# A transformer block on one core: output and second feed-forward products with tokens on the partitions, as seven block products, and normalizations along rows

## What is computed

```python
mixed = (g_pool * y_pool + g_rwkv * y_rwkv) @ w_out[l]
x = layer_norm(ALPHA * x + (1 + gt1) * mixed, ln1_g[l], ln1_b[l], LN_EPS).astype(x.dtype)
h = x * (1 + sc2) + sh2
f = jnp.square(jax.nn.relu(h @ w_ff1[l])) @ w_ff2[l]
x = layer_norm(ALPHA * x + (1 + gt2) * f, ln2_g[l], ln2_b[l], LN_EPS).astype(x.dtype)
```

## Time and profile before

| | us |
|---|---|
| median of 3 runs | 1109.46 |
| range of the runs | 1108.66 to 1114.62 |
| profiled execution | 1106.47 |
| its span, first to last instruction | 1104.7 |
| TensorE busy in the span | 999.9 |
| DVE, ACT, POOL busy | 517.9, 413.8, 401.8 |
| mean granted TensorE clock | 0.957 |

### The profile page before, as it was taken

How to read it: one execution, slowest core, us unless ns; L and a number is a source line. 1 busy time by engine, 2 the same in 40 slices (tenths; PEclk the granted TensorE clock), 3 DMA queues, 4 the chain that set the end, 5 groups by cost and what they waited for, 6 DMA issues and landing times.

```text
span 1104.7 us, 25425 instructions
## 1 busy us (share of the span) xinstructions
PE 999.9 (91%) x10997; PEld 798.8 (72%) x10997; DVE 517.9 (47%) x620; ACT 413.8 (37%) x500; POOL 401.8 (36%) x236
## 2 busy tenths in 40 slices
PE   1898998898899889997999999889999999999992
PEld 1676777685677678675688888768888888888881
DVE  6636589377748768743231245746112112112217
ACT  0335354356335532524433224375124224214311
POOL 6333412311311131125253443445434434443422
PEclk9799999999999899998899999879999999999996
DMA  9322333223323324321433543304333333333201
GB/s 370 106 77 63 97 117 102 79 79 94 93 79 98 103 60 118 105 76 39 133 100 101 160 114 107 95 1 132 97 94 97 96 96 91 99 95 93 79 1 76
DMA packets 153641, 108.08 MB, mean 98 GB/s; under 512 B 5395, under 2 KB 145601, under 8 KB 153537
## 3 DMA queue, kind: packets, MB, share of 16 engines
q1 hardware_dynamic: 143729, 83.46, 25.9%
q10 hardware_dynamic: 9808, 23.08, 6.9%
HBM read 100.23 MB, written 2.10 MB: 93 GB/s over the span
## 4 chain that ended last, share of the span: by engine, by line
PE 47%; DVE 4%; DMA 1%; ACT 1%; issue 0%; SPq 0%; POOL 0%; DVEq 0%; ACTq 0%; POOLq 0%
PE set L1757 23%; PE bank L1757 20%; PE bank L1859 1%; PE set L1859 1%; DVE G L1319 1%; DMA w_raw<-in_w_rwkv_up_dram 1%; DVE xt L1388 1%; DVE xt L1390 1%; PE set L1821 0%; DVE t L1304 0%; PE set L1838 0%; PE set L1607 0%; PE set L1606 0%; DVE aa L1322 0%; DVE stat L1348 0%
## 5 line engine op out<-in xcount | busy, mean ns | idle before, releaser
L560 POOL TENSOR_TENSOR w_lo<-w_raw,w_hi 128x1024 fp32r<-128x1024 f32 (+2 forms) x87 | 200.4, 2303 | 439.2 <-ACT w_hi L641 399.2
L616 POOL TENSOR_TENSOR w_lo<-w_raw,w_hi 128x1024 fp32r<-128x1024 f32 x48 | 115.8, 2413 | 145.9 <-ACT w_hi L936 145.7
L1460 PE MATMUL bank<-h_hi,w_hi 128*128 128x512 f32 x256 | 109.3, 427 | 2.1 <-POOL w_lo L560 2.0
L641 ACT ACTIVATE w_hi<-w_raw 128x1024 fp32r<-128x1024 f32 (+2 forms) x75 | 75.5, 1006 | 82.9 <-PE set L1757 43.6
L669 ACT ACTIVATE Q<-set 128x1024 f32<-128x1024 f32 x56 | 57.4, 1026 | 130.7 <-PE set L1514 73.8
L936 ACT ACTIVATE w_hi<-w_raw 128x1024 fp32r<-128x1024 f32 x60 | 63.7, 1061 | 110.7 <-PE bank L1757 53.9
L1460 PE MATMUL bank<-h_hi,w_lo 128*128 128x512 f32 x256 | 103.3, 403 | 0.3 <-issue 0.3
L1460 PE MATMUL bank<-h_lo,w_hi 128*128 128x512 f32 x256 | 103.5, 404 | 0.0
L1355 DVE TENSOR_TENSOR f<-t 128x512 f32<-128x512 f32 x32 | 26.4, 825 | 125.9 <-ACT t L945 125.5
L1757 PE MATMUL bank<-h_hi,w_hi 128*128 128x512 f32 x192 | 76.5, 398 | 0.0
L1757 PE MATMUL set<-y_hi,w_hi 128*128 128x512 f32 x192 | 76.1, 396 | 0.0
(11 more groups left out here) (328 smaller groups left out, 2030.3 us busy)
## 6 DMA issues: line engine op xcount, KB each, us to landing
w_raw<-in_w_ff_dram SPq DMA_DIRECT2D x64, 512.0 KB, 3.9
w_raw<-in_w_in_dram SPq DMA_DIRECT2D x46, 512.0 KB, 3.8
y<-in_w_ada_dram ACTq DMA_DIRECT2D x20, 512.0 KB, 4.0
ada<-in_w_ada_dram SPq DMA_DIRECT2D x16, 512.0 KB, 9.6
Q<-in_w_ada_dram ACTq DMA_DIRECT2D x12, 512.0 KB, 4.3
w_raw<-in_w_rwkv_up_dram SPq DMA_DIRECT2D x8, 512.0 KB, 4.3
w_raw<-in_w_out_dram SPq DMA_DIRECT2D x8, 512.0 KB, 3.8
xtok<-in_x_dram SPq DMA_DIRECT2D x4, 512.0 KB, 9.9
```

Source lines behind the costliest of these rows:

```text
L560: link(pool.tensor_tensor(part_of(k, w_lo), part_of(k, w_raw), part_of(k, w_hi).bitcast(F32), ALU.subtract), "lo_ready")
L616: again(pool.tensor_tensor(part_of(k, w_lo), part_of(k, w_raw), part_of(k, w_hi).bitcast(F32), ALU.subtract), "lo_ready")
L641: link(act.activation(part_of(k, w_hi), part_of(k, w_raw), ACT.Copy), "hi_ready")
L1460: mm = pe.matmul(o, w, hx, start=(m == 0), stop=(m == 3 * KT - 1))
```

## The change

**Seven products.** The output product and the second feed-forward product are cut into units of 512 rows of the contraction: two units for `w_out`, eight for `w_ff2`. In each the activations A (512 tokens x 512) and the weights B (512 x 1024) are taken as 2 x 2 blocks; eight block products become seven, of sums and differences of blocks (the form of Winograd). Tokens stand on the partitions of the result: the activations (`a_hi`, `a_lo`, 128 x 128 blocks) stand in TensorE, the weights move, 512 columns at a time. A form is 12 matmuls. DVE makes the sums of activations (`lows`) and of weights (`summed`), and adds every product from PSUM to `res` (`take`, 14 a unit). Some products are accumulated in a bank that has been read already, so that TensorE waits for the take of an earlier one (`FREED_BY`). ACT makes the high parts of the activations (`highs`).

**Gates in the weights.** `1 + gt1` and `1 + gt2` are spread over rows by 16 matmuls in the last pass of the scan (`spread_gate`), and DVE multiplies each weight quarter by them (`scaled`).

**Order.** Output unit 0 stands between `pool_up(5)` and `rwkv_up(6)`, unit 1 behind `pool_up(7)`. A feed-forward unit is four hidden chunks (24 matmuls each) and seven forms; units 1 to 7 are a loop on every engine. Its tiles share three slots of `w_hi` and `w_lo`.

**Normalizations.** Statistics, root and scaling run along rows for both. After LN1 the rows are transposed (32 transposes) for the hidden products. The residual for LN2 is scaled by rows of `ln1_g` and `ln1_b` on DVE and POOL. `x` is loaded in rows into `res`.

The diff, cut to its core:

```diff
+        FORMS = ("B11", "B21", "T2", "T1", "T3", "B22", "T4")
+        QUARTERS = dict(B11=(3, 0, 0), B12=(4, 0, 1), B21=(5, 1, 0), B22=(6, 1, 1))
+        FIRST_SLOT, SLOT = (1, 2, 0, 2, 0, 1, 2, 0, 1, 2, 0), (1, 2, 1, 2, 0, 1, 2, 0, 1, 2, 0)
+        BEFORE = (8 - PER, 9 - PER, 0, 1, 10 - PER, 2, 3, 4, 5, 6, 7)
+        PRODUCTS = ((0, 4), (2, 0), (5, 4), (4, 6), (1, 4), (6, 6), (3, 4))
+        OPENS = (True, True, False, True, False, False, False)
+        FREED_BY = (6, None, 0, 5, 2, 3, 4)
+        A_READY = ((1, 3), (2, 4), (5, 7), (5, 7), (6, 8), (6, 8), (6, 8))
...
# ACT, a unit of the loop
+            def highs(link, n, base, units=0, per=0):
+                i = n % 2
+                if n % 4 < 2:
+                    link(act.activation(a_hi[:, 0, i, :], left[:, i, 0:S // 2], ACT.Copy), "a_hi")
+                    act.wait_ge(sem("a_summed"), units * 4 + (n + 1))
+                    link(act.activation(a_hi[:, 1, i, :], a_sum[:, 0, :], ACT.Copy), "a_hi")
+                else:
+                    link(act.activation(a_hi[:, 2:4, i, :], halves(right[:, :]), ACT.Copy), "a_hi")
+                    act.wait_ge(sem("a_summed"), units * 4 + (n + 1))
+                    link(act.activation(a_hi[:, 4:7, i, :], a_sum[:, 1:4, :], ACT.Copy), "a_hi")
...
+                for m in range(2):
+                    split_again(again, m, q, 1)
+                for m in range(4):
+                    relu_of(again, m, q, 1)
+                    for k in {0: (2,), 1: (3, 4), 2: (5,), 3: (6,)}[m]:
+                        split_again(again, k, q, 1)
+                    highs(again, 12 + m, 0, q)
+                for m in range(7, PER):
+                    split_again(again, m, q, 1)
...
# DVE
+            def lows(link, n, units=0):
+                i = n % 2
+                x0, x1 = left[:, i, 0:S // 2], left[:, i, S // 2:S]
+                if n % 4 < 2:
+                    link(dve.tensor_tensor(a_sum[:, 0, :], x0, x1, ALU.subtract), "a_summed")
+                    dve.wait_ge(sem("a_hi"), units * 8 + (2 * n + 1))
+                    link(dve.tensor_tensor(a_lo[:, 0, i, :], x0, a_hi[:, 0, i, :].bitcast(F32), ALU.subtract), "a_low")
+                    dve.wait_ge(sem("a_hi"), units * 8 + (2 * n + 2))
+                    link(dve.tensor_tensor(a_lo[:, 1, i, :], a_sum[:, 0, :], a_hi[:, 1, i, :].bitcast(F32), ALU.subtract), "a_low")
+                else:
+                    link(dve.tensor_tensor(a_sum[:, 1, :], x1, right[:, S // 2:S], ALU.add))
+                    link(dve.tensor_tensor(a_sum[:, 2, :], a_sum[:, 1, :], x0, ALU.subtract))
+                    link(dve.tensor_tensor(a_sum[:, 3, :], right[:, 0:S // 2], a_sum[:, 2, :], ALU.subtract), "a_summed")
+                    dve.wait_ge(sem("a_hi"), units * 8 + (2 * n + 1))
+                    link(dve.tensor_tensor(a_lo[:, 2:4, i, :], halves(right[:, :]), a_hi[:, 2:4, i, :].bitcast(F32), ALU.subtract), "a_low")
+                    dve.wait_ge(sem("a_hi"), units * 8 + (2 * n + 2))
+                    link(dve.tensor_tensor(a_lo[:, 4:7, i, :], a_sum[:, 1:4, :], a_hi[:, 4:7, i, :].bitcast(F32), ALU.subtract), "a_low")
...
+                link(dve.tensor_tensor(two_by(w_raw[raw]), two_by(w_raw[raw]), row, ALU.mult), "summed")
...
+                link(dve.tensor_tensor(res[:, j, half], bank[PRODUCTS[at][1] + row], res[:, j, half], ALU.add), "taken")
...
+            def unit_sums(link, units):
+                for m in range(4):
+                    dve.wait_ge(sem("hidden_raw"), units * 4 + (4 + m + 1))
+                    lows(link, 12 + m, units)
+                    if m == 0:
+                        scaled(link, "B22", 3, units)
+                        scaled(link, "B21", 3, units)
+                    if m == 1:
+                        summed(link, "T1", 3, units)
+                        summed(link, "T3", 3, units)
+                    if m == 2:
+                        summed(link, "T2", 3, units)
+                    if m == 3:
+                        summed(link, "T4", 3, units)
...
+            with dve.Fori(0, NU - 2) as q:
+                again = loop_link(dve, counts, q, per, "dve_step")
+                unit_sums(again, q)
+                for at in range(NFORM):
+                    for row in range(2):
+                        take(again, 3, at, row, q)
+                    if at == 4:
+                        scaled(again, "B11", 4, q)
+                scaled(again, "B12", 4, q)
...
# TensorE
+                    for row in range(2):
+                        free(at, row)
+                        if at and FREED_BY[at] is not None and FREED_BY[at] < at:
+                            pe.wait_ge(sem("taken"), units * (2 * NFORM) + (2 * NFORM * unit + 2 * FREED_BY[at] + row + 1))
+                        for i in range(2):
+                            if row == 0:
+                                pe.wait_ge(sem("a_low"), units * 8 + (8 * unit + A_READY[form][i]))
+                            for m, (a, wx) in enumerate(((a_hi, w[0]), (a_lo, w[0]), (a_hi, w[1]))):
+                                mm = pe.matmul(bank[first + row], a[:, form, i, row * P:(row + 1) * P], wx[:, i, :],
+                                               start=OPENS[at] and i == 0 and m == 0, stop=i == 1 and m == 2, skip_group_check=True)
```

More of the change, by code:

```diff
@@ L966, in _ @@
+            rounds_done(counts, {"hi_ready": PER, "relu": 4, "hidden_raw": 4, "a_hi": 8}, NU - 1)
+            root(0, 1)
+            normalise(0, 1)
+            normalise(1, 1)
+            root(1, 1)
         @block.vector
@@ new lines, in _ @@
+                raw = left[:, n % 4, :] if n % 4 < 2 else right[:, :]
+                link(dve.tensor_tensor(raw, right[:, :], f2[:, :], ALU.add), "mix_sum")
+                if n not in (KT - 4, KT - 3):
+                    lows(link, n)
+                if n == KT - 5:
+                    dve.wait_ge(sem("gate_rows"), 2)
+                    for name in ("B11", "B12", "B22", "B21"):
+                        scaled(link, name, 0)
+                if n == KT - 4:
+                    for name in ("T1", "T3"):
+                        summed(link, name, 0)
@@ new lines, in _ @@
+                if n == KT - 3:
+                    summed(link, "T4", 0)
+                    dve.wait_ge(sem("res_ready"), TB)
+                    for at in range(NFORM):
+                        for row in range(2):
+                            take(link, 0, at, row)
+                    lows(link, KT - 4)
+                    lows(link, KT - 3)
+                    scaled(link, "B11", 1)
+                    scaled(link, "B12", 1)
+                if n == KT - 2:
+                    scaled(link, "B22", 1)
+                    scaled(link, "B21", 1)
+                    for name in ("T1", "T3"):
+                        summed(link, name, 1)
@@ new lines, in _, with residual @@
+            scaled(link, "B11", 2)
+            scaled(link, "B12", 2)
+            scaled(link, "B22", 2)
+            scaled(link, "B21", 2)
+            dve.wait_ge(sem("rows_scaled"), 1)
+            def residual(z):
+                half = slice(z * S, (z + 1) * S)
+                for j in range(2):
+                    link(dve.tensor_tensor(res[:, j, half], res[:, j, half], ln_rows[:, 0, half], ALU.mult))
+                    link(dve.tensor_tensor(res[:, j, half], res[:, j, half], ln_rows[:, 1, half], ALU.add))
@@ new lines, in hidden_chunk @@
+            def hidden_chunk(m, slot, units, base):
+                k = K_FF + base * PER + m
+                pe.wait_ge(sem("lo_ready"), units * PER + (k + 1))
+                for kt in range(KT):
+                    for at, (w, hx) in enumerate(((w_hi, h2_hi), (w_hi, h2_lo), (w_lo, h2_hi))):
+                        mm = pe.matmul(bank[m][:, :], w[slot][:, kt, :], hx[:, kt, :], start=(kt == 0 and at == 0),
+                                       stop=(kt == KT - 1 and at == 2))
+                mm.then_inc(sem("w_used"), 1)
@@ new lines, in _, with ff_free, free @@
+            for m in (2, 3):
+                hidden_chunk(m, FIRST_SLOT[m], 0, 0)
+            def ff_free(unit, units, base):
+                def free(at, row):
+                    if at == 0:
+                        pe.wait_ge(sem("taken"), units * (2 * NFORM) + (2 * NFORM * (unit - 1) + 2 * 6 + row + 1))
+                    elif at == 1:
+                        pe.wait_ge(sem("relu"), units * 4 + (4 * base + row + 1))
+                    elif at == 3:
+                        pe.wait_ge(sem("taken"), units * (2 * NFORM) + (2 * NFORM * (unit - 1) + 2 * 5 + row + 1))
+                return free
```

734 lines of the change are left out of this document (414 added, 320 removed).

## The result

The changed kernel takes 1199.15 us (median; 1192.54 to 1204.14) where the kernel before takes 1109.06: a ratio of 1.080, 95% interval 1.074 to 1.087. It is slower, as forecast, by 90 us instead of 57. The time lies 33 us above the forecast and 4 us above the top of the range. The profiled execution is the fastest of the four, 1192.54 us with a span of 1190.6.

The account below looks back on a forecast made before the run. DVE and POOL, excluding each other on SBUF reads, were taken to bound the loop. Output end 706.7, first unit 73, seven units 366 and tail 16 gave span 1161.8, execution 1163.6, median 3.0 more: 1166 us, range 1125 to 1195.

Parts of the forecast that it names:

- DVE and POOL take turns: DVE instructions with both inputs in SBUF and POOL subtractions exclude each other whole; some 13 us of DVE waits per unit.
- the saving of matmuls: Output and second feed-forward products: 120 fewer matmuls, 27.6 us; a feed-forward unit 41.4 instead of 44.2 if TensorE sets pace.
- The first feed-forward unit: From the last output product to this unit's end: 73 us, with the third form at 58.
- The slow clock of a loop unit: Behind the 6 us wait in each loop unit, matmuls start 0.43 us apart at first, adding some 0.7 us.
- The tail: After the last unit: takes, statistics, root, three rows on DVE and one on POOL, store; 16 us against 22.
- Rival 1: DVE's waits fall into its idle time, TensorE keeps the pace, units stay near 43 us: 1075 us; chance 0.12.
- rival 4: Forms with tokens standing and weights moving take over 0.230 us a matmul; 3% more adds 8 us; chance within any.
- Rival 2: Milder: DVE wins the port twice more in a unit, units of 47 to 48 us, 1125 to 1140; chance 0.07.
- Rival 3: Worse: POOL slips in before T4, +2.3, or clock stays 1.2 GHz through two forms, +4; 1185 to 1200; chance 0.11.
- end of output unit 1: Unit 0, four up products and unit 1 sum to 77.5 us, ending at 706.7 against 705.6 today.
- seven units: Loop units 1 to 7 of the feed-forward stage: 52.3 us each, 366 together, 8.1 a unit over today's 44.2.
- The early part: To the end of pool_up(4): earlier weight loads and gate matmuls in TensorE's wait give minus 3 us (0 to -6).

Follow-up runs that it names:

- filled gaps: Changed kernel plus 25 and 11 dummy matmuls in TensorE's two waits of each loop unit: 1192.6 us.
- second profile: The changed kernel run once more with nothing edited, for another profile of it: 1198.8 us.
- the experiment on the loads: Kernel before, with the first three weight chunks of the second up product loaded ahead of the pooling tiles: 1109.5 us, ratio 1.0004.
- all waits gone: Changed kernel with POOL's loop subtractions cut to 128 of 1024 elements and three reorderings of DVE and ACT instructions: 1118.2 us.
- the best order: Changed kernel with T4 later, B22, T1 and T3 earlier, and the last chunk's high halves ahead of T2's copy, nothing left out: 1154.9 us.

## Why the forecast was right in kind and short in size

**The bound and the mechanism** were right: DVE and POOL take turns, TensorE waits twice a unit, and the saving of matmuls is lost. **What failed are three terms of the sum.** The first feed-forward unit was priced with DVE's scalings and residual products free of POOL, at 10.5 us, where they took 20.4 (term 73, measured 83.3). The slow clock of a loop unit was put at 0.7 us and took 2.0. The tail was priced free of POOL as well, at 16, and took 20.8. Rival 1, TensorE keeping the pace at 1075 us, is refuted, and so is rival 4, as the 84 matmuls take 0.23 us each. Rival 2 is refuted by the units. Rival 3 in its first form (POOL slips in before T4) didn't happen, T4 took 1.22 to 1.23 us in all seven units; its second (the clock stays low longer) did, with 1.3 us a unit instead of 4. The time fell into the span given for it (1185 to 1200), but mostly through other terms.

Term by term, on the profiled execution (span forecast 1161.8, measured 1190.6, 28.8 more):

| term | forecast | measured | difference |
|---|---|---|---|
| end of output unit 1 | 706.7 | 705.0 | -1.7 |
| from there to the end of the first feed-forward unit | 73 | 83.3 | +10.3 |
| seven units | 52.3 each | 54.5 each | +15.4 |
| tail | 16 | 20.8 | +4.8 |

**The seven units.** The chain on DVE was worked out to within 1 us: the first take ended at 38.6 us of the unit against 37.75, the third form began at 38.7 against 37.8. That is 0.9 of the 2.2 us. The other 1.3 are the term with the slow clock. "4 to 6 us of work brought it back" gave 0.7 us, and it was 2.0 (15.8 instead of 13.8). Of these 2.0, 0.3 stand at full clock too (14.1 us with the filled gaps). By the prediction's own chain its 0.7 would have fallen into the wait for the first take, ahead of the third form; what counts is how slow the five forms behind it are. The row it was taken from, 723 to 735 us of the earlier trace rows, had TensorE at work at once. In the unit it works 4 us and waits again for the bank (1.09 us), and the clock was 0.61 on average over 11.2 us. The Trainium skill (TensorE: Matmul & The Clock Gate, HAM oscillation) warns of a loop that starts each round at the lower clock; the trace agrees in part: in the second profile the five forms took 14.1 us in three of six units, as with filled gaps at a clock of 1.00, and 15.6 to 15.8 in the other three.

**The first feed-forward unit** missed most for its length. The forecast priced 4 scalings, 4 products and 4 additions on DVE as if alone (10.5 us). The scalings took 7.9 us, the first four of the products and additions 7.7 and the other four, from 767.0 on, 4.8, together 20.4. The third form of this unit began 67.7 us behind the last output product, where 58 was forecast:

```profile
706.72 1.96 DVE L1484 SCALAR_TENSOR_TENSOR small<-small 128x2 f32<-128x2 f32 x1
...
725.71 7.93 DVE L1428 TENSOR_TENSOR w_raw<-w_raw,gate 128x1024 f32<-128x1024 f32 x4
733.67 1.67 DVE L1562 TENSOR_TENSOR res<-res,ln_rows 128x512 f32<-128x512 f32 x1
```

It had counted POOL's work there (10 us) without applying to it the rule that it had just derived. Taking POOL's residual products away gives 6.8 to 10.6 us back, shortening its tiles 10.7 to 14.5. They were not taken away together, so whether the two add up is not shown. The first line is part of the normalization, forecast at 10 and measured at 13.3 us (first hidden product at 718.3). An instruction of two elements waits for POOL's whole tile like any other.

**The tail**, forecast by sums of free instructions, was short for the same reason. DVE in order of time at the end:

```profile
1174.45 1.62 DVE L1478 TENSOR_SCALAR small<-small 128x2 f32<-128x2 f32 x1
1176.47 0.17 DVE L1483 RECIPROCAL small<-small 128x2 f32<-128x2 f32 x1 [0.40 <-ACT small L1021]
1176.67 1.81 DVE L1484 SCALAR_TENSOR_TENSOR small<-small 128x2 f32<-128x2 f32 x1
1178.51 1.28 DVE L1616 SCALAR_TENSOR_TENSOR res<-res,small,ln_rows 128x1024 f32<-128x1024 f32 x1
```

Two instructions on two elements wait 1.45 and 1.65 us for POOL, which works on the row of token block 0 beside them: 3.1 of the 4.8 us. The rest lies in the order of the last additions and statistics.

**The early part.** The forecast gave 3 us to the loads and the gates' place. From the last attention output to the end of pool_up(4) it was 116.6 us before (from 515.6), 112.1 in the first profile after, but 116.2 in the second. The clock of the last attention products accounts for the 4.5 us (5.4 us at 1.00 against 10.1 at 0.50, and 9.3 in the second profile), and the experiment on the loads found nothing. So the forecast's gain is not shown, and the match of 705.0 with 706.7 is luck: in the second profile output unit 1 ends at 713.8. This also explains why the median lies 6.6 us above the profiled execution, where the forecast had added 3: the second profile is 6.2 us longer in span, 8.2 more ahead of output unit 0, 3.6 more in the stretch behind it, and 5.6 less after that, by the faster units. In the attention products and in the first feed-forward unit the granted clock goes with the difference; why it is granted in one execution and not in the other is open, and so are 4.1 us ahead of the last attention output.

**Could the change have paid?** With all waits gone the loop's seven units give 7 x (44.2 - 41.95) = 16 us, and the whole kernel took 1118. If its start and its first unit had been the shortest ones seen (635.0 and 142.6 us instead of 645.3 and 156.6), its span would be 1116.2 - 10.3 - 14.0 = 1092 against 1104.7, an estimate from two kernels that leave low parts out. Against that 1% stand DVE's 18.2 us of instructions with two SBUF inputs (27.9 busy less 14 additions of 0.69) and POOL's 27.5 per unit. One behind the other they are 45.7, already more than TensorE's 41.95. The forecast had that sum (44.8), and the best order came within 1 us of it, at 46.7. With the seven subtractions on DVE the sum is smaller, but DVE's own 39 us take over, and the units average 46.4. No version of the change that leaves nothing out beat the kernel before.

## What to carry to other kernels

Before trading matmuls for additions, add up the time of VectorE's instructions with two SBUF inputs and of GpSimd's reading ones, for each stage, as if they were one engine. If the sum exceeds what TensorE has left, the order can hide part of the loss and no more. Then walk the chain from the last product to the first addition out of PSUM, price each link at its value behind GpSimd, and apply that to every stage, the short ones at the beginning and the end too. A gain of a few us that stands on one profiled execution is worth a second profile before anything is built on it.

## What the runs showed of the hardware that was not expected

- A VectorE instruction on two elements per partition takes 1.62 to 1.96 us beside GpSimd's subtraction and 0.16 free. Its size doesn't protect it. One of them (L1478) has a single SBUF tensor as input.
- GpSimd's write of 128x896 (0.84 us) excludes nothing: VectorE's subtraction beside it took 0.43 us.
- The same loop unit took 52.85 or 54.5 us within one execution, by the granted clock alone (0.90 to 0.94 against 0.87 over the unit). The 73 matmuls at the end of the attention part took 5.4, 9.3 or 10.1 us at 1.00, 0.55 and 0.50: the difference is more than the 3 us that the forecast gave to the early part.
- Two ScalarE instructions in the other order (1.07 us) moved a unit by 2.3 us at the same clock, since they decided whether DVE or POOL went first.
